# Gated delta rule inside a three-layer fp32 forward pass: the inverse's first level reordered, weight splits placed differently, the SGU affine on VectorE, two narrow projections turned

## The reference

```python
# hybrid_mixer: x is (1, 256, 1024); PROJ_SIZES = (3072, 1024, 8, 8, 2048, 1024, 1024)
proj = jnp.einsum("bld,dp->blp", x, w_in)
qkv, z, a, b, uv, gate_dn, gate_sgu = jnp.split(proj, offsets, axis=-1)
q, k, v = jnp.split(jax.nn.silu(causal_depthwise_conv(qkv, conv_w)), 3, axis=-1)   # 8 heads of 128, q and k normalized
beta = jax.nn.sigmoid(b)
g = -jnp.exp(a_log) * jax.nn.softplus(a + dt_bias)
# gated_delta_rule, chunks of 64
a_mat = jnp.where(strict, einsum("bnhtk,bnhsk->bnhts", k_beta, k) * decay, 0.0) + jnp.eye(64)
u = solve(a_mat, v_beta)                       # triangular solve
w = solve(a_mat, k_beta * jnp.exp(g_cum)[..., None])
def step(state, inp):                          # scan over the 4 chunks
    v_new = u_c - einsum("bhtk,bhkv->bhtv", w_c, state)
    out = einsum("bhtk,bhkv->bhtv", q_c, state) + einsum("bhts,bhsv->bhtv", qk_c, v_new)
    state = state * gl_c[..., None, None] + einsum("bhsk,bhsv->bhkv", k_c, v_new)
# spatial_gating
u, v = jnp.split(jax.nn.gelu(uv, approximate=False), 2, axis=-1)
v = layer_norm_2(v, ln_g, ln_b)
gated = u * (einsum("gts,bnsgc->bntgc", w_causal, v) + spatial_b)
y = sigmoid(gate_dn) * (o @ w_dn_out) + sigmoid(gate_sgu) * (gated @ w_sgu_out)
# hierarchical_moe, its router (4 + 16 columns)
group_logits = t @ router_group_w + router_group_b
expert_logits = t @ router_expert_w + router_expert_b
```

## Time and profile before

| | |
|---|---|
| median of 3 runs | 1348.68 us (1343.44 to 1350.7) |
| the profiled execution's own time | 1343.33 us |
| its span, first to last instruction | 1341.6 us |
| TensorE busy, share of span | 1278.9 us, 95% |
| VectorE busy | 833.7 us, 62% |
| ScalarE busy | 601.7 us, 45% |
| GpSimd busy | 186.2 us, 14% |
| TensorE's mean granted clock | 0.978 |
| DMA | 205.02 MB, mean 153 GB/s |

### The profile page before, as it was taken

How to read it: one execution, slowest core, us unless ns; L and a number is a source line. 1 busy time by engine, 2 the same in 40 slices (tenths; PEclk the granted TensorE clock), 3 DMA queues, 4 the chain that set the end, 5 groups by cost and what they waited for, 6 DMA issues and landing times.

```text
span 1341.6 us, 20799 instructions
## 1 busy us (share of the span) xinstructions
PE 1278.9 (95%) x8994; PEld 1193.0 (89%) x8994; DVE 833.7 (62%) x972; ACT 601.7 (45%) x697; POOL 186.2 (14%) x140
## 2 busy tenths in 40 slices
PE   8999999999999999999998999899899999999996
PEld 7977999998998899998998988899898899999995
DVE  6566855558437765557586449753767675555554
ACT  4565433334654533335562447423733543333331
POOL 8300400004000400002303100120400040000002
PEclk9999999999999999999898989899899999999998
DMA  9712665554533465567894338732465356555550
GB/s 270 179 46 94 218 222 188 188 189 126 189 126 126 157 222 188 187 173 129 107 154 97 64 64 157 126 64 64 159 203 188 107 181 202 184 184 185 187 187 31
DMA packets 160220, 205.02 MB, mean 153 GB/s; under 512 B 13571, under 2 KB 142322, under 8 KB 160130
## 3 DMA queue, kind: packets, MB, share of 16 engines
q1 hardware_dynamic: 157906, 195.80, 52.5%
q0 software_dynamic: 2224, 7.90, 2.0%
HBM read 202.63 MB, written 1.05 MB: 152 GB/s over the span
## 4 chain that ended last, share of the span: by engine, by line
PE 81%; ACT 6%; DVE 5%; issue 2%; DMA 2%; SPq 2%; POOL 1%; POOLq 0%; DVEq 0%; ACTq 0%
PE PS L365 23%; PE PS L366 23%; PE PS L367 23%; ACT w_hi L1573 2%; DVE w_lo L1006 2%; PE PS L844 2%; ACT AR L1603 1%; PE PS L856 1%; PE PS L852 1%; DMA ring<-in_w_in 1%; SPq L2097 1%; SPq L2136 1%; POOL AR L2046 1%; DMA ring<-in_a_w_in 1%; DVE AR L1350 1%
## 5 line engine op out<-in xcount | busy, mean ns | idle before, releaser
L1006 DVE TENSOR_TENSOR w_lo<-ring,w_hi 128x2048 fp32r<-128x2048 f32 x182 | 436.8, 2404 | 235.0 <-ACT w_hi L1573 234.8
L365 PE MATMUL PS<-x_hi,w_hi 128*128 128x256 f32 x1648 | 478.7, 290 | 6.9 <-ACT AR L1585 2.3
L1573 ACT ACTIVATE w_hi<-ring 128x2048 fp32r<-128x2048 f32 x182 | 347.6, 1912 | 281.0 <-PE PS L367 265.4
L366 PE MATMUL PS<-x_lo,w_hi 128*128 128x256 f32 x1648 | 470.1, 285 | 0.0
L367 PE MATMUL PS<-x_hi,w_lo 128*128 128x256 f32 x1648 | 470.1, 285 | 0.0
L365 PEld LDWEIGHTS PS<-x_hi,w_hi 128*128 128x128 f32 x1648 | 320.3, 194 | 13.2 <-issue 5.7
L366 PEld LDWEIGHTS PS<-x_lo,w_hi 128*128 128x128 f32 x1648 | 320.3, 194 | 3.3 <-issue 1.7
L367 PEld LDWEIGHTS PS<-x_hi,w_lo 128*128 128x128 f32 x1648 | 319.8, 194 | 0.0
L1585 ACT ACTIVATE AR<-PS 128x512 f32<-128x512 f32 (+1 forms) x144 | 82.4, 586 | 300.2 <-PE PS L367 185.9
L365 PE MATMUL PS<-w_hi,o_hi 128*128 128x512 f32 x480 | 188.5, 393 | 0.8 <-ACT res L1585 0.8
L366 PE MATMUL PS<-w_lo,o_hi 128*128 128x512 f32 x480 | 187.4, 390 | 0.0
(11 more groups left out here) (372 smaller groups left out, 1406.9 us busy)
## 6 DMA issues: line engine op xcount, KB each, us to landing
ring<-in_mlp_w SPq DMA_DIRECT2D x64, 1024.0 KB, 5.2
ring<-in_w_in SPq DMA_DIRECT2D x32, 1024.0 KB, 9.5
ring<-in_expert_w_gate SPq DMA_DIRECT2D x16, 1024.0 KB, 5.4
ring<-in_expert_w_up SPq DMA_DIRECT2D x16, 1024.0 KB, 5.4
...
```

Source lines behind the costliest of these rows:

```text
L365: mm(out, a_hi, b_hi, start=first, stop=False, skip_group_check=True)
L366: mm(out, a_hi, b_lo, start=False, stop=False, skip_group_check=True)
L1006: v.tensor_tensor(w_lo[:, m % PARTS], ring[:, index[split[m]] % RING], w_hi[:, m % PARTS].bitcast(F32), ALU.subtract)\
L1573: a(w_hi[:, m % PARTS], ring[:, index[split[m]] % RING], ACT.Copy).then_inc(S("hi_split"), 1)
```

## The change

It does these things:

- First level: VectorE itself makes Bl of level 1 (signal `first_level`), right after the Ti starts and before the R starts; the Y products of level 1 wait for that alone, and the Tl and Rl products for the R starts (`inv_start`). GpSimd's masks begin at level 2. The `kt` results are read after level 1's updates. TensorE issues `kk` of both tiles, then `kq` of both, and takes 5 + 9 filler steps before the first level where it took 8 + 12. `turn` skips two banks before level 1's Tl and before level 2's Y.
- Splits: VectorE's `bank` and `read` from `ab` to level 2 run with `ahead` 1; in the scan with 0; after the scan one piece ahead. Around the SGU, VectorE and ScalarE split three ahead at named places, and ScalarE's copies of `uv` 0 and its splits stand between the Gelu, Sqrt and Sigmoid groups.
- SGU affine: two operations per tile on VectorE, (v - mean) x gain, then x 1/deviation + bias, in place of one on VectorE and two on GpSimd.
- Narrow projections: a/b and the router take the weights as the stationary operand and the 256 tokens as the moving one (24 products in place of 48), into banks `abT` and `rlT`; VectorE copies that to SBUF, and TensorE turns it (`by_tokens`) after four steps of the next piece.

```diff
-            def with_x(ps, name, t=None):
+            def with_x(ps, name):
                 pe.wait_ge(S("narrow_split"), 1 if name == "wga" else 2)
                 o, n = NARROW[name]
-                if t is None:
-                    for k in range(KT):
-                        c = slice(o + k * n, o + k * n + P)
-                        ins = products(ps, n_hi[:, c], n_lo[:, c], x_hi[:, k, :], x_lo[:, k, :], k == 0, k == KT - 1)
-                else:
-                    wh, wl, c = narrow_view(n_hi, name), narrow_view(n_lo, name), slice(t * P, (t + 1) * P)
-                    for k in range(KT):
-                        ins = products(ps, x_hi[:, k, c], x_lo[:, k, c], wh[:, k, :], wl[:, k, :], k == 0, k == KT - 1)
+                for k in range(KT):
+                    c = slice(o + k * n, o + k * n + ps.shape[0])
+                    ins = products(ps, n_hi[:, c], n_lo[:, c], x_hi[:, k, :], x_lo[:, k, :], k == 0, k == KT - 1)
+            def by_tokens(src, n, raw, pre, lo=0):
+                read_out(pe, raw)
+                ps = claim(pe, pre, nxt(lo, 8))
+                for t in range(TT):
+                    ins = nc.tensor.transpose(ps[:, t * 32:t * 32 + n], src[0:n, t * P:(t + 1) * P], ident[0:n, 0:n])
+                close(ins, pre)
...
                     by_feature(("q", 0))
-                    ps = claim(pe, "ab", nxt())
-                    for t in range(TT):
-                        ins = with_x(ps[:, t * 16:t * 16 + 16], "wsm2", t)
-                    close(ins, "ab")
-                    by_feature(("q", 1))
+                    ps = claim(pe, "abT", nxt())
+                    ins = with_x(ps[:, 0:T], "wsm2")
+                    close(ins, "abT")
+                    steps = triples(("q", 1), nxt())
+                    advance(steps, 4)
+                    by_tokens(s_abT, 16, "abT", "ab")
+                    advance(steps)
+                    steps = triples(("k", 0), nxt())
+                    advance(steps, 6)
                     pe.wait_ge(S("dn_gates"), 1)
...
-                    steps = triples(("k", 0), nxt())
-                    advance(steps, 6)
+                    advance(steps, 4)
                     gate_sums(0)
...
-                advance(fill, 8)
+                advance(fill, 5)
...
-                advance(fill, 12)
+                advance(fill, 9)
                 for l in range(1, LEVELS):
+                    if l == 2:
+                        turn[0] += 2
                     for t in range(TT):
-                        pe.wait_ge(S("level_mask"), (hb * (LEVELS - 1) + l - 1) * TT + t + 1)
                         if l == 1:
-                            pe.wait_ge(S("inv_start"), hb * TT + t + 1)
+                            pe.wait_ge(S("first_level"), hb * TT + t + 1)
                         else:
+                            pe.wait_ge(S("level_mask"), (hb * (LEVELS - 2) + l - 2) * TT + t + 1)
...
                     advance(fill, 4)
+                    if l == 1:
+                        turn[0] += 2
                     for t in range(TT):
                         read_out(pe, ("Yl", hb, l, t))
+                        if l == 1:
+                            pe.wait_ge(S("inv_start"), hb * TT + t + 1)
...
                 for t in range(TT):
-                    read(("at", hb, t))
-                    read(("kk", hb, t))
-                    for o, x, m in ((s_Ti, s_A, lvl0[:]), (s_R, s_B, lvl[:, 0])):
-                        ins = v.tensor_tensor(o[:, t], x[:, t], m.unsqueeze(1).broadcast_to([P, 4, P]), ALU.mult)
-                    after(ins)
-                    for o in (s_Ti, s_R):
-                        ins = v.scalar_tensor_tensor(o[:, t], o[:, t], -1.0, ident[:].unsqueeze(1).broadcast_to([P, 4, P]), ALU.mult, ALU.add)
+                    read(("kk", hb, t), 1)
+                    inverse_start(s_Ti, s_A, lvl0[:], t)
+                for t in range(TT):
+                    read(("at", hb, t), 1)
+                    v.tensor_tensor(s_Bl[:, t], s_B[:, t], four(lvl[:, 1]), ALU.mult).then_inc(S("first_level"), 1)
+                for t in range(TT):
+                    inverse_start(s_R, s_B, lvl[:, 0], t).then_inc(S("inv_start"), 1)
...
+                            ahead = PARTS - 1 if l > 2 else 1
...
-                    read(("U", hb, t))
+                    read(("U", hb, t), 0)
...
+                split_ahead(pieces_for[("ot", hb, NCH - 1)], 1)
             gated(1)
-            split_ahead(pieces_for[("uv", 0)])
+            split_ahead(pieces_for[("uv", 0)], PARTS)
...
-                v.tensor_scalar(u_v[:, t, :], u_v[:, t, :], st[:, 16 * t + 12:16 * t + 13], st[:, 16 * t + 15:16 * t + 16],
-                                ALU.subtract, ALU.mult).then_inc(S("sgu_normed"), 1)
+                ve.wait_ge(S("affine"), 32 * 5)
+                after(v.scalar_tensor_tensor(u_v[:, t, :], u_v[:, t, :], st[:, 16 * t + 12:16 * t + 13], res[:, 0, :], ALU.subtract, ALU.mult))
+                v.scalar_tensor_tensor(u_v[:, t, :], u_v[:, t, :], st[:, 16 * t + 15:16 * t + 16], res[:, 1, :], ALU.mult, ALU.add)\
+                    .then_inc(S("sgu_v"), 1)
```

93 lines of the change are left out of this document (51 added, 42 removed).

## The result

| | before | changed |
|---|---|---|
| median of the runs made together | 1349.69 us (1343.44 to 1354.09, 4 runs) | 1309.65 us (1306.53 to 1311.17, 4 runs) |
| the profiled execution | 1343.33 us, span 1341.6 | 1311.17 us, span 1309.4 |
| mean granted clock of TensorE in it | 0.978 | 0.987 |

The ratio is 0.9713 (95% interval 0.9679 to 0.9746): 2.9% faster, 40.0 us by the medians. The two profiled executions differ by only 32.2 us, because the one of before was among the fastest of its kernel and the one of the changed kernel was the slowest of its four. What follows goes by the traces.

The account below looks back on a forecast made before the run. TensorE, busy 95%, with its idle and low-clock stretches, was taken to bound the kernel. 15.9 + 7.7 + 7.1 + 4.3 + 3.6 + 1.3 - 0.9 = 39.0, less 2.0 for the clock, gave 37 us: 1309 us, range 1299 to 1325.

Parts of the forecast that it names:

- term 3: `uv` to `yd`: the first `yd` split comes earlier, so the idle 5.4 us and half-clock products go; 7.1 us gained.
- the 2.0 taken off for the clock: Whole kernel: allowance in us for the clock falling at the new waits of 1.4 to 2.7 us.
- Term 1: First level, both halves: Y waits only for VectorE's mask product and TensorE stops idling there; 15.9 us gained.
- The fear that GpSimd's masks of level 2 fall on the R starts: First level: the masks might double the R starts; bound of up to 2 us lost in each half.
- Terms 2 and 3: Scans: with nothing split there, the third chunks gain 5.5 + 2.3 us; `uv` to `yd`: 7.1 us gained.
- Term 4: a/b and router: 24 wide products replace 48, low clock goes; 4.3 (6.8 at full clock) + 3.6 us gained.
- It waits 1.4 us: Gates after a/b: TensorE wants them at 649.3, but they come at 650.6.
- some 2 us: Front of the delta block: expected wait at `qn` of pieces 0 and 1.
- rival A: Front of delta block bound by ScalarE-VectorE chain, clock falls at new waits: 24 us gained, 1319 to 1325; chance 0.15.
- Term 5: Banks: half 1 loses the `v` 3 wait, `qn` 2 takes `qn` 1's bank, 1.3 us gained; `uv` 0 loses 0.9.
- Rival D: Weight loads: slots come free up to one piece later, so the ring starves; slower, 1356 or more; chance 0.04.
- Rival E: Narrow projections: columns set the pace, so the wide form is dearer; 8 us less, 1317; chance 0.01.

Follow-up runs that it names:

- u_ahead: The changed kernel with only the splits in the delta inverse put back to two ahead, new order kept: ratio 0.9775, median 1312.91 us.
- u_level: The changed kernel with only the first level's order undone, its mask product back on GpSimd, splits still one ahead: ratio 0.9849, median 1324.15 us.
- u_scan: The changed kernel with only the splits inside the scan put back to two ahead: ratio 0.9848, median 1321.06 us.
- u_tail: The changed kernel with the old order of u copies and splits at the delta block's end, affine still on VectorE: ratio 0.975, median 1314.18 us.
- u_affine: The changed kernel with only the affine of the SGU put back on GpSimd: ratio 0.9723, median 1310.84 us.
- u_narrow: The changed kernel with only the two narrow projections back in their old form of 48 products: ratio 0.9825, median 1321.15 us.
- n_psum: As n_bank, with VectorE's sum ahead of the gates reading its first operand from PSUM instead of SBUF: ratio 0.9678, median 1303.79 us.
- n_bank_gate: As n_bank, with the gate sums asked for 6 filler steps later: ratio 0.9682, median 1305.22 us.
- n_bank: The changed kernel with the bank rotation moved on by two ahead of the second pair of norm sums, both halves: ratio 0.9682, median 1305.24 us.

## Why the prediction was right, and where its steps were off

The forecast was 1309 us within 1299 to 1325, and 1309.65 was measured. The main mechanisms held; that the two figures agree within 1 us is luck. 1309 was taken between two bases, 1306.3 off the profiled execution of before and 1311.7 off its median. On the first base 37 us were forecast and 32.2 came, on the second 37 were forecast and 39.0 came; the executions of before alone spread over 10 us. In the traces the parts that changed gave 34.8. Nearly every miss had one sign: 0.5 us more than forecast at term 3, less at a/b, the router and half 1, and the 2.0 taken off for the clock covered a part of it.

| term | forecast | traces |
|---|---|---|
| 1, first level, half 0 and 1 | 8.3 + 7.6 | 29.1 - 18.6 - 2.2 = 8.3; 28.4 - 18.6 - 2.2 = 7.6 |
| 2, scans | 5.5 + 2.3 | 5.5 + 2.3 |
| 3, `uv` to `yd`, with the bank of `uv` 0 | 7.1 - 0.9 | 45.0 - 40.4 + 2.2 = 6.7 (before rounding) |
| 4, a/b and the front of half 0 | 4.3 less a part of 2.0 | 71.7 - 69.0 = 2.7 |
| 4, router | 3.6 | 2.8 |
| 5, front of half 1 | +1.3 | 61.7 - 65.3 + 2.2 = -1.4 |

*Term 1.* The count held nearly to the row. VectorE's last of the mask products was forecast to end at 704.8, the last R start at 707.4; here they are (the whole trace stands 0.1 us earlier at this place):

```profile
703.25 1.28 DVE L1412 TENSOR_TENSOR AR<-AR,lvl 128x512 f32<-128x512 f32 x2
...
706.50 0.69 DVE L1401 SCALAR_TENSOR_TENSOR AR<-AR,ident 128x512 f32<-128x512 f32 x1
```

They end at 704.5 and 707.2; TensorE's first Y starts at 705.5. The fear that GpSimd's masks of level 2 fall on the R starts did not come true: the first began at 706.7 and it was the split behind the starts that took 3.1 us instead of 2.3. In u_ahead, where the starts come later, it did: the last one took 1.66 and 1.53 us, beside GpSimd's masks, instead of 0.68 and 0.69. What the text did not say, and u_level and u_ahead show, is how the gain divides: 11.4 for the order, 5.3 for the splits, counted to the end of the inverse.

*Terms 2 and 3* were right in mechanism and size. u_scan and u_tail confirm the mechanisms by undoing, at 10.2 and 6.5 us in the traces, and costing the affine at nothing was right (u_affine).

*Term 4* was right in its main step, that the load of the stationary sets the pace and that the low clock belongs to the narrow products (u_narrow). Two of its sizes were off. "It waits 1.4 us" at the gates was 2.2. Two errors lie in it: the copy of a/b came 1.1 us earlier than forecast, seen from the layer norm, and the chain behind it took 2.0 longer than in the trace of before, by the sum that met GpSimd's operation; without that the wait is gone (n_psum). And the "some 2 us" at `qn` 0 did not appear in the changed kernel, because TensorE had lost them at the gates; they appeared as 3.2 as soon as the gates were covered (n_bank_gate). The front of the block is bound by ScalarE and VectorE, as rival A had it, but its loss of 13 us did not follow: level 1 lost nothing by it, and in the delta block the clock fell behind two waits only. That the place still gained 2.7 us, with 2.2 of waiting and 3.1 of low clock against the 6.8 at full clock, is owed to a wait of 1.3 us for a split before `v` 0 (at 669.46 in before) that went too, and that the prediction does not name. At the router 0.9 us is a low clock behind the layer norm (1018.14 above).

*Term 5* failed. The step was that half 1 would gain 1.3 us because `v` 3's bank is no longer in the way and `qn` 2 then waits as the sum of old durations says. Both waits hang on the same engine, and that engine on a load: with the wait for `v` 3 gone TensorE only arrived earlier, and ScalarE read `qn` 1 no sooner. So 3.3 us of idle time ahead of the sums, 0.9 among them and 1.1 of half clock behind took the place of 2.3, 1.0 and 0.6. n_bank shows that it was the choice of bank: with another one 3.4 us of it go (0.6 come back up to level 2).

The 2.0 us taken off for the clock were too few: it cost 3.1 behind the gates (against n_bank), 1.1 at `qn` 2 and 0.9 behind the layer norm. It did so in this execution; that n_bank had the first wait without the fall shows how uncertain such a term is. Rival D (the ring starves) did not come, though the seed of it is there, 5 us of waiting for a load on ScalarE in half 1, as before the change. Rival E is excluded by u_narrow: the narrow form was slower at both places.
